# Seven block products for eight in the gate and up projections of a two-layer fp32 model

## The reference

```
hn2 = rmsnorm(x, norm2_w)
gu  = hn2 @ w_gate_up                       # 256 x 2048 by 2048 x 11264
x   = x + (silu(gu[..., :5632]) * gu[..., 5632:]) @ w_down
```

## Time and profile before

| | us |
|---|---|
| median of 3 runs | 2597.43 (2597.39 to 2597.46) |
| span of the profiled execution, first to last instruction | 2596.1 |
| around the span, up to the median of the runs | 1.3 |
| PE, busy in the span | 2587.4 |
| ACT | 1407.5 |
| POOL | 1207.3 |
| DVE | 1134.8 |

### The profile page before, as it was taken

One profiled execution on the slowest core, in us unless ns is written; L12 is line 12 of the kernel. 1 busy time (PEld: TensorE's weight loads), 2 busy tenths in 40 slices (PEclk: granted clock), 3 DMA queues, 4 the chain that ended last, 5 costly groups with the idle time before them and its releaser, 6 DMA issues.

```text
span 2596.1 us, 30138 instructions
## 1 busy us (share of the span) xinstructions
PE 2587.4 (100%) x11860; PEld 2145.5 (83%) x11860; DVE 1134.8 (44%) x1327; ACT 1407.5 (54%) x1729; POOL 1207.3 (47%) x528
## 2 busy tenths in 40 slices
PE   9999999999999999999999999999999999999999
PEld 7888888888888888888888888888888888888887
DVE  6798955434442232323333476456533232322222
ACT  7767654445555555555544574565555555555333
POOL 2687743344444444444444455333444444444443
PEclk9999999999999999999999999999999999999999
DMA  8767554476666666666666644553666666666554
GB/s 303 225 201 213 178 186 162 152 231 211 203 195 214 203 205 204 204 207 204 206 210 208 220 163 162 180 191 134 184 203 205 205 203 208 204 209 203 202 203 146
DMA packets 174700, 516.08 MB, mean 199 GB/s; under 512 B 108027, under 2 KB 111068, under 8 KB 117216
## 3 DMA queue, kind: packets, MB, share of 16 engines
q1 hardware_dynamic: 174128, 513.64, 61.0%
q10 hardware_dynamic: 432, 0.52, 0.1%
HBM read 487.38 MB, written 2.10 MB: 189 GB/s over the span
## 4 chain that ended last, share of the span: by engine, by line
PE 95%; DVE 1%; issue 1%; POOL 1%; ACT 1%; DMA 0%; SPq 0%; ACTq 0%; DVEq 0%; POOLq 0%
PE PB L774 30%; PE PB L778 30%; PE PB L775 29%; PE PB L1012 1%; PE PB L854 0%; PE PB L884 0%; POOL WL L3034 0%; PE PB L792 0%; PE PB L1117 0%; PE PB L972 0%; PE PB L894 0%; DVE WL L2069 0%; POOL HSD L3051 0%; ACT WH L1299 0%; PE PB L747 0%
## 5 line engine op out<-in xcount | busy, mean ns | idle before, releaser
L3034 POOL TENSOR_TENSOR WL<-RAW,WH 128x1024 fp32r<-128x1024 f32 x440 | 1083.8, 2464 | 1368.9 <-ACT WH L1299 1368.8
L1299 ACT ACTIVATE WH<-RAW 128x1024 fp32r<-128x1024 f32 x888 | 937.2, 1058 | 1070.5 <-PE PB L778 1059.7
L2069 DVE TENSOR_TENSOR WL<-RAW,WH 128x1024 fp32r<-128x1024 f32 x446 | 609.4, 1366 | 1371.6 <-ACT WH L1299 1371.4
L774 PE MATMUL PB<-WH,HNH 128*128 128x512 f32 x2432 | 956.3, 393 | 0.2
L778 PE MATMUL PB<-WL,HNH 128*128 128x512 f32 x2432 | 947.4, 390 | 1.5 <-POOL WL L3034 1.5
L775 PE MATMUL PB<-WH,HNL 128*128 128x512 f32 x2432 | 946.6, 389 | 0.0
L778 PEld LDWEIGHTS PB<-WL,HNH 128*128 128x128 f32 x2432 | 456.4, 188 | 99.3 <-POOL WL L3034 3.9
L774 PEld LDWEIGHTS PB<-WH,HNH 128*128 128x128 f32 x2432 | 456.6, 188 | 97.2 <-issue 3.0
L775 PEld LDWEIGHTS PB<-WH,HNL 128*128 128x128 f32 x2432 | 456.7, 188 | 93.0
L774 PE MATMUL PB<-WH,HDH 128*128 128x512 f32 x704 | 273.9, 389 | 0.0
L775 PE MATMUL PB<-WH,HDL 128*128 128x512 f32 x704 | 273.9, 389 | 0.0
(11 more groups left out here) (388 smaller groups left out, 1992.2 us busy)
## 6 DMA issues: line engine op xcount, KB each, us to landing
RAW<-in_w_gu SPq DMA_DIRECT2D x176, 1024.0 KB, 4.8
RAW<-in_w_dn SPq DMA_DIRECT2D x88, 1024.0 KB, 4.8
RAW<-in_w_in_a SPq DMA_DIRECT2D x53, 1024.0 KB, 5.3
RAW<-in_w_in SPq DMA_DIRECT2D x45, 1024.0 KB, 4.8
RAW<-in_w_out SPq DMA_DIRECT2D x32, 1024.0 KB, 4.8
RAW<-in_w_ga SPq DMA_DIRECT2D x24, 1024.0 KB, 4.8
RAW<-in_w_gb SPq DMA_DIRECT2D x24, 1024.0 KB, 4.8
WIN<-in_win SPq DMA_DIRECT2D x8, 512.0 KB, 5.7
```

Source lines behind the costliest of these rows:

```text
L774: e.matmul(o, hi[:, k, x], WH[:, s, c], start=k == 0, stop=False)
L1299: e.activation(WH[:, u % NSPL, :], RAW[:, n % NRAW, half * SU * 128:(half + 1) * SU * 128], ACT.Copy).then_inc(*wt.act.mark(("wh", u)))
L2069: e.tensor_tensor(to, raw, hi, ALU.subtract).then_inc(*wt.dve.mark(("wl", u)))
L3034: e.tensor_tensor(to, raw, hi, ALU.subtract).then_inc(*wt.pool.mark(("wl", u)))
```

## The change

In groups 1 to 10 of each layer, k tiles 0 to 7 are multiplied as blocks. For `d` in 0 and 1, raw unit `d` of gate and raw unit `d` of up are a 2 x 2 matrix of blocks, with two k tiles by 512 columns each: `b11` and `b21` are the two halves of gate, `b12` and `b22` those of up. The tokens are a 2 x 2 matrix too, halves of the tokens by pairs of k tiles. Of these, seven products are made for eight, with sums of blocks on both sides (Strassen in Winograd's form):

- Sums of the tokens (`row_sums`, once a layer, in group 0's second half): DVE forms `HNS = HNH + HNL` and four sums `SAF`, ACT rounds them to `SAH`, DVE makes the remainders `SAL`.
- Sums of the weights (`weight_sum`, DVE, in place in the `RAW` buffers): `t1 = b11 + b12`, `t2 = t1 + b22`, `t3 = t2 - b11`, `t4 = t2 + b21`, each before its own split into high and low. The seven blocks `b11, b21, b22, t1, t2, t3, t4` are each rounded by ACT. POOL makes the remainders of blocks 0, 3 and 5, DVE those of 1, 2, 4 and 6.
- On PE (`summed_group`) each of the seven blocks goes with one half of the tokens: 6 matmuls. Over both `d` the products collect in seven PSUM banks. K tiles 8 to 15 follow as before; gate's and up's products for them are added straight onto four of the banks.
- Sums of the products on DVE: `products_summed` (four of 128x512, out of PSUM) after the summed half, `gate_summed` (two) before silu, `up_summed` (two) at the end of the group, then the product of gate and up, which now has both inputs in SBUF. ACT copies one bank to SBUF and takes silu from SBUF.
- The order of raw units becomes gate, up, gate, up in these groups (`gate_up_order`). There are four raw buffers and six slots for rounded and remainder halves there, in space that `HDH` and `HDL` leave unused until then. A block is prepared five units ahead of its use.
- The transposes of the hidden activations are issued 16 tiles later, with one target buffer. The splits, joins and transposes stay in the groups; `rounded` and `remainder` move to the end of group 10 (`j` 0 and 1) and into the first group of the down projection.

The core of the diff:

```
+BLOCKS = ("b11", "b21", "b22", "t1", "t2", "t3", "t4")
+BANK_OF = (1, 2, 3, 5, 6, 7, 4)
+BY_POOL = (0, 3, 5)
+SUM_BEHIND = {0: 3, 2: 4, 3: 5, 4: 6}
+STARTS = {(32 * i + 6) // 7: i for i in range(7)}
...
+            if s > 10:
+                tile = max(tile, splits[s - slots + 1][1], first - 24 if slots == NSPL else 0)
+                due.setdefault(tile, []).append(key)
...
+                for d in range(2):
+                    for n in w.tiles(32):
+                        if n not in STARTS:
+                            continue
+                        i = STARTS[n]
+                        key, q = (stage, j, d, i), BANK_OF[i]
...
+                        e.wait_ge(*wt.act.done("wh", *key))
+                        for r in range(2):
+                            (hi, lo), c = left(i, d, r), slice(r * 512, (r + 1) * 512)
+                            e.matmul(banks[q][:, :], hi, wh(key)[:, c], start=d == 0 and r == 0, stop=False)
+                            e.matmul(banks[q][:, :], lo, wh(key)[:, c], start=False, stop=False)
+                            if r == 0:
+                                e.wait_ge(*low_half(*key))
+                            t = e.matmul(banks[q][:, :], hi, wl(key)[:, c], start=False,
+                                         stop=d == 1 and r == 1 and q not in (2, 3, 4))
+                        t.then_inc(*wt.pe.mark(("unit", *key)))
...
+                if BLOCKS[i] == "t2":
+                    e.wait_ge(*low_half(*s, 2))
+                    e.wait_ge(*wt.dve.done("sum", *s, 3))
+                    e.tensor_tensor(b22, b12, b22, ALU.add).then_inc(*wt.dve.mark(("sum", *s, i)))
+                if BLOCKS[i] == "t3":
+                    e.wait_ge(*low_half(*s, 0))
+                    e.wait_ge(*wt.dve.done("sum", *s, 4))
+                    e.tensor_tensor(b11, b22, b11, ALU.subtract).then_inc(*wt.dve.mark(("sum", *s, i)))
...
+                    for key in due.get(w.i - 1, ()):
+                        low(*key)
+                        if len(key) > 1 and key[3] in SUM_BEHIND:
+                            weight_sum(*key[:3], SUM_BEHIND[key[3]])
```

More of the change, by code:

```diff
@@ L367, in build @@
         order += [("w_out2", i) for i in range(16)]
[L368 to L386, removed]
+        order += [("w_gu2", i) for i in gate_up_order()] + [("w_dn2", i) for i in range(44)]
@@ new lines, in build @@
+        both_halves = order.index(("w_in2", 4))
+        summed, wider = {}, set()
+        for stage, name in ((1, "w_gu"), (3, "w_gu2")):
+            for j in range(1, 11):
+                for d in range(4):
+                    n = order.index((name, 8 * j + d))
+                    wider.update((n, n + 1))
+                    if d < 2:
+                        summed[n] = stage, j, d
+        splits = []
+        for n, (name, i) in enumerate(order):
+            slots = NSPL + MORE if n in wider else NSPL
+            if n in summed:
+                splits += [((*summed[n], i), 16 * n + t, slots) for t, i in STARTS.items()]
+            elif n - 1 not in summed and name != "w_cmp":
+                splits += [((2 * n + half,), 16 * n + 8 * half, slots) for half in range(2)]
@@ new lines, in build @@
+        slot, slot_before, due, tile = {}, {}, {}, 0
+        held = [(-1, None)] * (NSPL + MORE)
+        for s, (key, first, slots) in enumerate(splits):
+            place = min(range(slots), key=lambda p: held[p][0])
+            slot[key], slot_before[key] = place, held[place][1]
+            held[place] = s, key
+            if s > 10:
+                tile = max(tile, splits[s - slots + 1][1], first - 24 if slots == NSPL else 0)
+                due.setdefault(tile, []).append(key)
+        raw_place, raw_count, raw_before, raw_due = {}, {}, {}, {}
@@ new lines, in sums_rounded @@
+                def sums_rounded():
+                    e.wait_ge(*m.dve.done("sums made", stage))
+                    for c in range(2):
+                        x, y = (flat4(z[:, 2 * c:2 * c + 2, :, :]) for z in (SAH, SAF))
+                        e.activation(x, y, ACT.Copy).then_inc(*m.act.mark(*([("sums", stage)] if c else [])))
+                for k in tiles(64):
+                    if k == 4 and stage == 1:
+                        x_normed(stage, gain, 2)
+                    if k == 18:
+                        normed_turned(stage, gain, 3)
+                        token_squares(stage, ("x", before), 3)
+                    if k == 40:
+                        token_root(stage)
```

404 lines of the change are left out of this document (301 added, 103 removed).

## The result

The changed kernel takes 2851.0 us (median of 4 runs, 2846.4 to 2852.9) against 2597.4 beside it: 1.097 times the time before [1.096, 1.099]. The forecast was 2739 with a range of 2655 to 2825. The direction was right, the size was not: 112 us more than forecast, and above the range. The execution shown here has a span of 2848.6 us, 252.5 more than before.

The account below looks back on a forecast made before the run. SBUF access shared by DVE and POOL bounds the group: 46.5 us plus gaps of 3.1 and 0.8 make 50.4, 6.9 more than now. Over 20 groups 138, plus 4 for entries and exits, on 2596.1: predicted 2739, range 2655 to 2825.

Parts of the forecast that it names:

- The bound: Groups 1 to 10: DVE and POOL take turns on one SBUF access, in use 46.5 us a group.
- rival of separate engines: Summed operations on DVE and POOL don't hold each other; PE stays the bound at 40.8 us, 2543 to 2560; chance 0.08.
- What is removed: Summed half on PE: 12 matmuls fewer a group, 2.72 us, 54.4 us over 20 groups.
- Gap 1: Near a group's end: gate sums, silus and a rounding leave the access idle 3.1 us.
- gap 2: Second summed d: the split into planes on ACT precedes POOL's rounding; about 0.8 us idle.
- The two transposes: On the load queue between two raws, 6.5 us, joins late: costed at nothing, 8 to 10 us of slack.
- the end of the group: Up sums wait for PE's last matmul, the seventh block's remainder behind them: no more cost.
- The bank: Third block's PSUM bank, freed only by the first up sum: its matmuls have slack before the next starved unit.
- More gaps: Sums wait singly, or ACT's splits, joins and copies fall badly: 54.6 us a group, 2819; chance 0.11.
- The clock falls: PE's waits in the summed half drop its clock from 2.4 to 1.2 GHz: some 2929; chance 0.04.
- Half of it: Turns of DVE and POOL overlap enough for a period of about 43.5 us: 2597; chance 0.03.
- access without gaps: DVE and POOL always find work, 46.5 us a group: 2657, with entries 2661; chance 0.14.

Follow-up runs that it names:

- e1: Changed kernel with POOL's three remainder blocks of the summed half moved to DVE: 2715.5 us.
- h1: Changed kernel with silus later, up sums and sums of products earlier, split at tile 6, transposes at tile 12, no POOL remainders in groups 1 to 10: 2608.1 us.
- f2: Changed kernel with the silus at tiles 121 and 123 for 117 and 119, behind the rounding of the fourth summed block: 2787.0 us.
- g1: Changed kernel with the split into planes at tile 2 and the transposes at tile 12, ahead of the waiting load: 2797.7 us.
- h3: Changed kernel with silus later, up sums and sums of products earlier, split at tile 6, transposes at tile 12, POOL's share kept: 2741.8 us.
- e2: Changed kernel with the two up sums made at tile 118, ahead of DVE's remainder and last weight sum there: 2819.9 us.
- e3: Changed kernel with DVE's sums of products at tiles 82 to 87 and ACT's joins at 90 and 98, both later: 2799.6 us.
- f1: Changed kernel with the split of the planes at tile 10 for 30 and the transposes at 20 for 44: 2834.8 us.

## Why the prediction was right and wrong

**The bound, right.** "SBUF access common to DVE and POOL", 46.5 us a group: 46.1 to 46.4 measured in every variant that keeps POOL's share and the sums, whatever the order, 40.0 with the three blocks moved, 38.1 without the sums. The rival of separate engines is refuted by e1: moving work onto the busier engine made the kernel 135 us faster. The remainders behind a POOL turn are recorded at 3.42 us, one POOL turn of 2.33 and one DVE turn of 1.1. The signs named for this came too: from 880 to 1290 us DVE's remainders and sums take 2.1 us in the mean (near 2 forecast) and POOL's remainders 2.8 (near 2.9). The Trainium skill ("SBUF — State Buffer", Who interferes with whom) gives the lock for the whole instruction; by that rule the trace agrees, at the 3.42 us.

**What is removed, right in kind.** 240 matmuls fewer (11,620 for 11,860), 54 us of PE. PE is no longer the bound, so none of it reaches the time. In h1, where PE is nearly the bound again, the group takes 43.33 us and not 40.8: 1.7 us are waits in the summed half, the other 0.8 I can't put down to one thing.

**Gap 1 and gap 2, right.** 3.1 and 0.8 forecast, 3.02 and 0.49 measured, both at the named places; f2 takes the first one down to 1.19.

**The step that failed.** "The two transposes (6.5 us) stand on the same queue between two raws; their joins come late in the group. I cost them at nothing, with 8 to 10 us of slack." They cost 4.13 and 2.54 us in turn, and 1.07 for the sums of products behind them. I had counted from the tile at which they are issued (44), not from the moment at which SP comes to them: the load ahead of them waits for the last block of the summed pair. I had taken their time to landing as that of one alone, where the queue was held 7.39 us by the pair. And I had left out that DVE's sums of products wait for them too. g1 and h3 show it: with the transposes ahead of the waiting load the stretch is gone, in h3 with the split behind its input no new one of 3.1 us takes its place, and in both ACT's joins and these sums wait for no transpose. It is the wait that the prediction named as a sign that it would be wrong. The second term is the end of the group, "costs no more": the up sums run with POOL idle, 1.20 us, since POOL's next rounding comes late. Together with the short starts: 20 x (9.5 - 3.9 - 0.2) = 108 of the 112 us, in which 0.2 is what the use came out below 46.5. About 6 us outside the groups for 4, and about 1 us by which the runs' median lies further above the span than taken, are the rest.

**The bank, right though the trace seems to say otherwise.** "Its matmuls have slack" was right: PE's waits there are put down to L3088, and e2 takes all of them away (95 us) and gains about the access' idle 1.2 us a group. Its "none in the other half" was not quite right: PE waits there for DVE's remainders, 11.4 us in the 410 of the window (L924).

**More gaps** (2819, 54.6 us a group for the 55.8 measured) came nearest of the rivals. It named ACT's joins at a bad place among its mechanisms, and that is one of the stretches found; the single waits of the sums, its other one, weren't found. **The clock falls** didn't happen as priced, 2929, but the granted clock did fall, to 0.966 over the span, another of the prediction's signs of being wrong: there were short stretches at the lower level (below), while the access was the bound. **Half of it** and **access without gaps** are refuted by the use and idle of the table.

## What to carry to other kernels

Where two engines share an access, add up their turns as one engine, and then find the stretches in which neither has work: here the turns gave the forecast's 46.5 us and kept it through every change of order, and each engine's busy share (66% and 49%) gives nothing. The idle stretches are what an order can win; the turns only a move of work between the two. An instruction in an in-order queue is as early as the instruction ahead of it that waits longest; before a transfer or a helper step is costed at nothing, find the waiting instruction it stands behind, and what stands behind it in turn. An idle stretch that is removed pays only until the next late thing in the same queue: e3 gave 51 of 105 us expected.

## What the runs showed of the hardware that I had not expected

- Two DMA transposes of the hidden planes hold SP's queue for 7.4 us (7.39, 7.54, 7.17, 7.96 in four kernels; 5.27 in f1 and 5.47 in the kernel before), and a load behind them isn't issued before. What makes the difference wasn't tested.
- PE's clock falls for moments. The timeline of PE in the changed kernel behind the wait for a bank:
```profile
970.58 0.79 PE L901 MATMUL PB<-WH,SAH 128*128 128x512 f32 x1 [4.95 <-DVE UPS L3088]
971.17 0.63 PE L902 MATMUL PB<-WH,SAL 128*128 128x512 f32 x1
971.60 0.63 PE L905 MATMUL PB<-WL,SAH 128*128 128x512 f32 x1
972.03 0.63 PE L901 MATMUL PB<-WH,SAH 128*128 128x512 f32 x1
```
Starts lie 0.43 us apart for 0.227, the lower of the two levels, 1.2 GHz, after PE had waited 4.95 us. The mean granted clock of the stage is lower than before, where it was 1.00. One window of the changed kernel (length, busy us of PE, PEld, DVE, ACT, POOL; clock):
```profile
880.00:1290.00 410.00, 330.28 (x1339) 260.63 (x1340) 342.82 (x220) 205.82 (x213) 207.40 (x75) 0.92 0.49 167
```
In h1, where PE waits 13.2 us in 340, it is 1.00. In e2, whose waits for the up sums' bank are gone but not the others, it is 0.93. The Trainium skill ("TensorE: Matmul & The Clock Gate", HAM oscillation) tells of the low clock coming back with waits; this case shows it. That it cost no time is argued and not tested: none of the long idle stretches of the access ends with PE.
- A product with both inputs in SBUF takes 0.70 us alone and was recorded at 4.46 for two when it fell behind a POOL turn (f2): in the common access an operation of half the size pays the whole turn of the other engine.
